# Five more expert blocks computed ahead, the decays behind two rows, the attention heads in two rounds: five reorderings in a two-block transformer kernel

## The reference, cut to what matters

```python
def first_block(x, c, ...):                      # windowed attention + gated linear attention, then PEER
    x = x + gate1 * mixed
    h2 = rms_norm(x, norm2_w) * (1 + scale2) + shift2
    x = x + gate2 * peer_ffn(h2, peer_wq, peer_subkeys, peer_u, peer_v)
    return rms_norm(x, final_norm_w)

def peer_ffn(h, wq, subkeys, u, v):              # 16384 experts, 8 heads, top 16 each
    q = (h @ wq).reshape(B, S, 8, 2, 128)
    sub_scores = einsum('bshpk,hpnk->bshpn', q, subkeys)
    top_v, top_i = top_k(sub_scores, 16)         # per half; sums of pairs; top 16 of 256; softmax = gates
    hid = gelu(einsum('tkd,td->tk', u[expert], x)) * gates
    return einsum('tk,tkd->td', hid, v[expert])

def second_block(x, c, ...):
    x = x + 0.5 * gt1 * swiglu(modulate(x, ...), w1_gate, w1_up, w1_down)
    proj = modulate(x, ...) @ w_in
    y_mla = softmax(mask(q k^T + q_pe k_pe^T)) v @ w_o_mla        # 8 heads, 512 x 512, causal by chunks of 64
    y_gdn = gated_delta_rule(silu(conv(q, k, v)), a, b, z) @ w_o_gdn   # decays from a, b; 8 chunks of 64
    x = x + gt2 * ((gate_mla * y_mla + gate_gdn * y_gdn) @ w_out)
    x = x + 0.5 * gt3 * swiglu(modulate(x, ...), w2_gate, w2_up, w2_down)
    return rmsnorm(x, g_final)
```

## Time and profile before

| | |
|---|---|
| median of three runs | 3515.35 us (3514.06 to 3519.29) |
| profiled execution | 3512.49 us, span of the trace 3510.7 us |
| mean granted TensorE clock | 0.962 |
| busy share of TensorE, VectorE, ScalarE, GpSimd | 94, 58, 38, 15% |
| chain that ended last | TensorE 82%, VectorE 10%, ScalarE 4%, DMA 2%, GpSimd 2% |

### The profile page before, as it was taken

The page is one execution under the profiler, slowest core; times in us unless marked ns, Lnnn a source line. Parts: engine busy times, 40 slices in busy tenths (PEclk is TensorE's granted clock), DMA queues, the critical chain, the costliest instruction groups (busy, mean ns, idle before and its releaser), DMA issues.

```text
span 3510.7 us, 41073 instructions
## 1 busy us (share of the span) xinstructions
PE 3300.3 (94%) x16321; PEld 2728.8 (78%) x16321; DVE 2047.9 (58%) x3543; ACT 1326.3 (38%) x2337; POOL 528.5 (15%) x547
## 2 busy tenths in 40 slices
PE   8999979999999999999999987989898998899998
PEld 5755879998888888888788866778687655678887
DVE  5765987867778888777555335535533344433332
ACT  3131238973444444444322234445442123232221
POOL 0001009962222222221000000000000000000000
PEclk9998999999999999999899998999898999999999
DMA  6416234669999899886355321122121121222222
GB/s 249 145 60 222 73 115 149 220 229 344 322 329 329 318 331 326 323 322 218 123 187 183 134 99 49 64 81 78 54 82 54 38 100 48 90 70 99 96 95 74
DMA packets 188767, 572.45 MB, mean 163 GB/s; under 512 B 16416, under 2 KB 80672, under 8 KB 170272
## 3 DMA queue, kind: packets, MB, share of 16 engines
q1 hardware_dynamic: 150704, 365.99, 29.8%
q0 software_dynamic: 37872, 203.84, 15.9%
HBM read 522.91 MB, written 46.86 MB: 162 GB/s over the span
## 4 chain that ended last, share of the span: by engine, by line
PE 82%; DVE 10%; ACT 4%; DMA 2%; POOL 2%; issue 1%; SPq 0%; DVEq 0%; ACTq 0%; POOLq 0%
PE ps L231 11%; PE ps L232 11%; PE ps L233 11%; PE ps L1601 5%; PE ps L1602 5%; PE ps L1600 5%; PE ps L240 4%; PE ps L1362 4%; PE ps L1364 4%; PE ps L1363 4%; PE ps L581 2%; PE ps L316 2%; DVE Wl L223 1%; PE ps L171 1%; DMA hidden_dram<-peerg_HS 1%; PE ps L584 1%
## 5 line engine op out<-in xcount | busy, mean ns | idle before, releaser
L223 DVE TENSOR_TENSOR Wl<-W,Wh 128x1024 fp32r<-128x1024 f32 x363 | 438.4, 1208 | 697.5 <-ACT Wh L217 697.5
L217 ACT ACTIVATE Wh<-W 128x1024 fp32r<-128x1024 f32 x363 | 377.7, 1041 | 567.0 <-PE ps L233 545.0
L1362 PE MATMUL ps<-peer_Hh,Wh 128*128 128x384 f32 x1024 | 348.9, 341 | 14.1 <-DVE Wl L223 14.1
L1364 PE MATMUL ps<-peer_Hh,Wl 128*128 128x384 f32 x1024 | 345.2, 337 | 0.0
L1363 PE MATMUL ps<-peer_Hl,Wh 128*128 128x384 f32 x1024 | 344.8, 337 | 0.0
L1570 POOL DMA_INDIRECT peerv_UV<-peer_uv,peer_EX x128 | 210.0, 1640 | 655.8 <-DVE peer_Y L1637 606.4
L1600 PE MATMUL ps<-peerv_VH,peer_HTh 128*128 128x512 f32 x768 | 299.9, 391 | 8.2 <-DVE peer_HTl L1663 8.2
L1602 PE MATMUL ps<-peerv_VH,peer_HTl 128*128 128x512 f32 x768 | 301.2, 392 | 0.0
L1601 PE MATMUL ps<-peerv_VL,peer_HTh 128*128 128x512 f32 x768 | 301.2, 392 | 0.0
L231 PE MATMUL ps<-f_Hh,Wh 128*128 128x512 f32 x672 | 262.3, 390 | 2.2 <-DVE Wl L223 2.2
L233 PE MATMUL ps<-f_Hh,Wl 128*128 128x512 f32 x672 | 261.5, 389 | 0.0
(11 more groups left out here) (490 smaller groups left out, 6508.9 us busy)
## 6 DMA issues: line engine op xcount, KB each, us to landing
W<-peer_u SPq DMA_DIRECT2D x128, 512.0 KB, 7.0
peerv_VR<-peer_v SPq DMA_DIRECT2D x128, 512.0 KB
gates_dram<-peerg_GB SPq DMA_DIRECT2D x12, 2048.0 KB, 7.3
peerv_GR<-gates_dram SPq DMA_DIRECT2D x32, 768.0 KB, 8.8
f_AW<-w_ada POOLq DMA_DIRECT2D x48, 512.0 KB, 4.3
W<-w_gate SPq DMA_DIRECT2D x44, 512.0 KB, 3.2
W<-w_up SPq DMA_DIRECT2D x44, 512.0 KB, 3.2
swa_AW<-w_ada POOLq DMA_DIRECT2D x32, 512.0 KB, 4.4
```

Of the source, the lines that this page charges most:

```text
L217: A.then_inc(e.activation(w_parts(i)[0], w_raw(i), ACT.Copy), ("w_hi", i))
L223: V.then_inc(e.tensor_tensor(lo, w_raw(i), hi.bitcast(F32), SUB), ("w", i))
L1362: e.matmul(o, hi[:, k, :], H2[0][:, k, 0:TD], start=k == 0, stop=False)
L1364: ins = e.matmul(o, lo[:, k, :], H2[0][:, k, 0:TD], start=False, stop=k == 7)
```

## The change

It does seven things. (1) `NPRE` becomes 54 and `FIRST` 15; 32 blocks stay between the one-hot products and 7 follow at the end. (2) VectorE's split of expert tiles 1 and 2 moves from the gates stage into the last two steps of the query stage, and the two `behind(e, "query")` go. (3) At the start of the dense stage SP's first two `gr_load` and GpSimd's first three gathers stand ahead of `hidden_written`. (4) The transposes of the decays and what follows on ScalarE and VectorE move behind the first two rows; the splits of row 1 move ahead of the decays. (5) The `uq` fills move one place back, and the eighth goes to `BEHIND`. (6) In the heads, VectorE's five steps are cut in two rounds, and each round has a piece of 6, 6, 3, 6 or 3 matmuls of a branch tile. (7) The first two tiles of `w_out` run their parts 0 to 6 first and part 7 last, each part behind its own wait.

```diff
-    NPRE = 49
+    NPRE = 54
-    NQ, FIRST = 96, 12
+    NQ, FIRST, EARLY = 96, 15, 2
@@ def query_dve(e):
-            if nb < 15:
+            if nb < 15 + EARLY:
                 w_lo(e, (t_q + t_u)[nb + 2])
@@ def gates_dve(e):
-        behind(e, "query")
+        PE.wait_ge(e, ("sub", 15))
         for p in range(FIRST):
-            w_lo(e, t_u[p + 1])
+            if p >= EARLY:
+                w_lo(e, t_u[p + 1])
@@ def dense_sp(e):
         gates_written(e)
-        hidden_written(e)
         gr_load(e, 0)
         gr_load(e, 1)
+        hidden_written(e)
@@ def dense_pool(e):
         gates_written(e)
-        hidden_written(e)
         for k in range(128):
+            if k == 3:
+                hidden_written(e)
             uv_load(e, k)
@@ mix2_pe, mix2_act, mix2_dve: the transposes and all behind "tcv" go into decay_pe, decay_act, decay_dve
+        w_hi(e, t_row[1])
+        w_lo(e, t_row[1])
@@ def rows_pe(e):
                 pe_three(e, ps(n % 2), t_row[n], 8, 128, H4, 0, 8, ("row", n))
+            if n == 1:
+                decay_pe(e)
@@ def rows_act(e): (rows_dve likewise, with w_lo and decay_dve)
-            if n < NROW - 1:
+            if 0 < n < NROW - 1:
                 w_hi(e, t_row[n + 1])
+            if n == 1:
+                decay_act(e)
@@ def delta_pe(e): (the waits of delta_act and delta_dve for "nds" and "tcv" go too)
-        V.wait_ge(e, "tcv")
-        A.wait_ge(e, "tcv")
@@ FILL
-            ([("rope", 0)], [("red", 0), ("bc", 0), ("uq", 0)]),
-            ([("uq", 1), ("on", 0)], [("ot", 0, 0), ("uq", 2)]),
+            ([("rope", 0)], [("red", 0), ("bc", 0)]),
+            ([("uq", 0), ("on", 0)], [("ot", 0, 0), ("uq", 1)]),
...
+        def pieces_pe(self, e, nb):
+            n = len(self.banks)
+            if nb >= n:
+                V.wait_ge(e, (self.tag, "out", nb - n))
+            V.wait_ge(e, ("w", self.ts[nb]))
...
+            for ks in ((0, 1), (2, 3), (4,), (5, 6), (7,)):
+                for k in ks:
+                    e.matmul(o, hi[:, k, :], self.parts[0][:, k, :], start=k == 0, stop=False)
+                    e.matmul(o, hi[:, k, :], self.parts[1][:, k, :], start=False, stop=False)
+                    ins = e.matmul(o, lo[:, k, :], self.parts[0][:, k, :], start=False, stop=k == 7)
+                if k == 7:
+                    PE.then_inc(ins, ("w", self.ts[nb]), (self.tag, "t", nb))
+                yield
@@ def attend_dve(e, h):
             V.then_inc(e.tensor_scalar(st[:, 1:2], st[:, 0:1], -SC_, None, MUL), ("pneg", h, q))
+            yield
             A.wait_ge(e, ("pexp", h, q))
             V.then_inc(e.reciprocal(st[:, 3:4], st[:, 2:3]))
             V.wait_ge(e, V.n)
             P = P_[:, q % 2, 0:w_]
             V.then_inc(e.tensor_scalar(P, P, st[:, 3:4], None, MUL), ("pn", h, q))
-            yield
@@ def branch_pe(e):
-        for r in range(39):
-            if r % 5 == 3:
-                br1.tile_pe(e, r // 5)
-            yield
+        for nb in range(8):
+            for _ in br1.pieces_pe(e, nb):
+                yield
@@ def wout2_pe(e):
-        V.wait_ge(e, ("y", "lo", 7))
-        for nb in range(8):
+        for t, k in [(t, k) for k0 in (0, 7) for t in (0, 1) for k in (range(7) if k0 == 0 else (7,))]:
+            V.wait_ge(e, ("y", "lo", k))
...
+            if k == 7:
+                PE.then_inc(ins, ("w", t_wo2[t]), ("wout2", t))
+        for nb in range(2, 8):
```

More of the change, by code:

```diff
@@ L1955, in mix2_pe, with decay_pe @@
         n4.pe_two(e, [ps(2), ps(3)], t_ab, 8, [("ab", 0), ("ab", 1)])
+    def decay_pe(e):
         V.wait_ge(e, "lx")
@@ L1962, in mix2_pe, with decay_act, decay_dve @@
         PE.then_inc(ins, "tcv")
+    def decay_act(e):
+        PE.wait_ge(e, "tcv")
+        V.wait_ge(e, "tcv")
+        pv = ps(4).rearrange("p (b s h) -> p b s h", b=4, s=16)
+        A.then_inc(e.activation(tcv[:, :, 2, :], pv[:, :, 0, :], ACT.Exp))
+        A.then_inc(e.activation(tcv[:, :, 3, :], pv[:, :, 2, :], ACT.Exp), "tcv")
+    def decay_dve(e):
+        PE.wait_ge(e, "tcv")
+        pv = ps(4).rearrange("p (b s h) -> p b s h", b=4, s=16)
+        V.then_inc(e.tensor_copy(tcv[:, :, 0:2, :], pv[:, :, 0:2, :]), "tcv")
+        V.wait_ge(e, "tcv")
+        V.then_inc(e.tensor_scalar(nds8, tcv[:, :, 0, :], -1.0, None, MUL), "nds")
     def mix2_act(e):
@@ L1976, in mix2_act @@
         A.then_inc(e.activation(ea[0:8, 0:1], vec("a_log")[0:8, :], ACT.Exp), "ea")
-        PE.wait_ge(e, "tcv")
-        V.wait_ge(e, "tcv")
-        pv = ps(4).rearrange("p (b s h) -> p b s h", b=4, s=16)
-        A.then_inc(e.activation(tcv[:, :, 2, :], pv[:, :, 0, :], ACT.Exp))
-        A.then_inc(e.activation(tcv[:, :, 3, :], pv[:, :, 2, :], ACT.Exp), "tcv")
     def mix2_dve(e):
@@ L2005, in mix2_dve @@
                                    SQc[:, :, 63:64].broadcast_to([8, 8, 64]), SQc, SUB), "lx")
-        PE.wait_ge(e, "tcv")
-        pv = ps(4).rearrange("p (b s h) -> p b s h", b=4, s=16)
-        V.then_inc(e.tensor_copy(tcv[:, :, 0:2, :], pv[:, :, 0:2, :]), "tcv")
-        V.wait_ge(e, "tcv")
-        V.then_inc(e.tensor_scalar(nds8, tcv[:, :, 0, :], -1.0, None, MUL), "nds")
     def part(h, c):
@@ L2087, in rows_dve @@
         for n in range(NROW + 2):
-            if n < NROW - 1:
+            if 0 < n < NROW - 1:
                 w_lo(e, t_row[n + 1])
+            if n == 1:
+                decay_dve(e)
             if n - 2 in norm_of:
@@ L2332, in delta_pe @@
     def delta_pe(e):
-        V.wait_ge(e, "tcv")
-        A.wait_ge(e, "tcv")
         row_steps(chain(rows_pe(e), keys_pe(e)), lambda h: head_pe(e, h))
     def delta_act(e):
-        V.wait_ge(e, "nds")
         x_out.wait_ge(e, "x")
@@ L2402, in build @@
             ([("uk", 6)], [("lsq", 0), ("uk", 7)]),
[6 rows of a table removed]
-    BEHIND = [("red", 3), ("uq", 8), ("uv", 0), ("on", 3), ("uq", 9), ("rope", 1), ("uv", 1), ("ot", 3, 0), ("ot", 3, 1),
+            ([("rope", 0)], [("red", 0), ("bc", 0)]),
+            ([("uq", 0), ("on", 0)], [("ot", 0, 0), ("uq", 1)]),
+            ([("uq", 2)], [("ot", 0, 1), ("red", 1), ("uq", 3)]),
+            ([("uq", 4), ("on", 1)], [("ot", 1, 0)]),
+            ([("uq", 5)], [("red", 2), ("ot", 1, 1)]),
+            ([("uq", 6), ("on", 2)], [("ot", 2, 0), ("ot", 2, 1)])]
+    BEHIND = [("red", 3), ("uq", 7), ("uq", 8), ("uv", 0), ("on", 3), ("uq", 9), ("rope", 1), ("uv", 1), ("ot", 3, 0), ("ot", 3, 1),
               ("uv", 2), ("uq", 10), ("rope", 2), ("uv", 3), ("uq", 11), ("rope", 3), ("uv", 4), ("uv", 5), ("rope", 4),
@@ L2663, in tile_pe @@
             pe_three(e, self.bank(nb), self.ts[nb], 8, 128, self.parts, 0, 8, (self.tag, "t", nb))
+        def pieces_pe(self, e, nb):
[3 more added lines that the diff above has]
+            V.wait_ge(e, ("w", self.ts[nb]))
+            hi, lo = (w.rearrange("p (k m) -> p k m", k=8) for w in w_parts(self.ts[nb]))
+            o = self.bank(nb)
+            for ks in ((0, 1), (2, 3), (4,), (5, 6), (7,)):
[6 more added lines that the diff above has]
+                yield
         def tile_act(self, e, nb):
@@ L2851, in wout2_pe @@
     def wout2_pe(e):
-        V.wait_ge(e, ("y", "lo", 7))
-        for nb in range(8):
+        w = [[x.rearrange("p (k m) -> p k m", k=8) for x in w_parts(i)] for i in t_wo2[0:2]]
+        for i in t_wo2[0:2]:
+            V.wait_ge(e, ("w", i))
+        for t, k in [(t, k) for k0 in (0, 7) for t in (0, 1) for k in (range(7) if k0 == 0 else (7,))]:
+            V.wait_ge(e, ("y", "lo", k))
+            o, (hi, lo) = ps(t), w[t]
+            e.matmul(o, hi[:, k, :], YP[0][:, k, :], start=k == 0, stop=False)
+            e.matmul(o, hi[:, k, :], YP[1][:, k, :], start=False, stop=False)
+            ins = e.matmul(o, lo[:, k, :], YP[0][:, k, :], start=False, stop=k == 7)
+            if k == 7:
+                PE.then_inc(ins, ("w", t_wo2[t]), ("wout2", t))
+        for nb in range(2, 8):
             if nb >= 4:
```

## The result

The changed kernel takes **3464.47 us** (median, 3460.65 to 3467.54) against 3514.7 us for the kernel before on the same chip: ratio **0.9856**, 95% interval 0.9839 to 0.9873. The forecast was 3460. The profiled execution took 3464.78 us, span 3463.0. So the total came out 4.5 us above the forecast, but its parts did not all come out, as the following shows.

What follows compares the result with a forecast made beforehand. TensorE was taken as the bound, with only its waits and low clock to remove. The terms -16 - 7 - 5 - 25 - 2.5 = -55.5 us gave 3457 profiled, 3460 us median; range 3447 to 3478, about 8 in 10.

Steps and rivals of the forecast that it cites:

- The bound: Whole kernel: the time is TensorE's own work, its waits and its low clock; the edits remove only waits and slow stretches.
- Parts 1 to 3: Gates and dense stage: blocks moved -20.9, gates' end +8.4, gates' start +3.7, dense start -7.2; -16.0 us, between -7 and -22.
- part 3: Dense start: earlier gathers and gate load leave a wait of 3 in place of 8.2 and no clock loss; -7.2 us.
- Part 4: Decays: two rows under the 11.75 us wait let row 2 start 8.4 us sooner; -7 us, between -3 and -9.
- The sign that the prediction asked for here: Decays: row 2 would stand about 8 us after the transposes of the decays.
- Part 5: `uq` fill: the 6.4 us wait on `QL` leaves 2.8 and the clock loss shrinks; -5 us (-2 to -6.5).
- Part 6: Heads: waits from VectorE's order get covered by the other head's maximum and branch matmuls; -25 us, bounds -11 and -31.
- Part 7: `w_out`: TensorE starts 2.7 us sooner, clock 1.5 kept, new wait of 1.7; net -2.5 us (-5 to +1).
- A: Rival, heads: TensorE's gain is half, through forty switches between kinds of matmul and semaphores; 3472 us, chance 0.16.
- B: Rival, gates: they only shift, the start slips by 8 us and the dense-start gate load stays late; 3470, chance 0.09.
- C: Rival, dense stage: VectorE or a landing stretches pairs of rounds, so TensorE no longer bounds; mostly near 3480, chance 0.05.
- D: Rival: a moved wait binds elsewhere; decays, `uq` fill and `w_out` give 4 in place of 14.5; 3470, chance 0.08.

Runs made afterwards that it cites:

- x4: The kernel before with only the first three parts (54 blocks ahead, early split, loads ahead of the writes' wait): 3499.69 us, 0.9956.
- x9: The kernel before with only the dense stage's loads of gates and expert rows ahead of the wait for the hidden rows' writes: 3505.0 us, 0.9974.
- x7: The changed kernel with 63 expert blocks ahead instead of 54: 3463.77 us, 0.9857 against the kernel before.
- x10: The kernel before with only the early split of the first two tiles and the later start of the list: 3507.23 us, 0.9982.
- x2: The kernel before with only the decays moved behind two rows: 3510.41 us, 0.9994.
- x5: The kernel before with only VectorE's head work in two rounds, branch tiles whole: 3510.99 us, 0.9991.
- x6: The kernel before with only the branch's tiles in pieces, VectorE's head work in one round: 3487.72 us, 0.993.
- x11: The changed kernel with row 0's convolution ahead of the decay chain and w_out's first two tiles one after the other: 3454.87 us, 0.9831 against the kernel before.
- x1: The changed kernel with the move of the decays undone: 3465.48 us, 0.9862 against the kernel before.
- x8: The changed kernel with row 0's convolution ahead of VectorE's decay chain and the decays' transposes behind row 2: 3461.33 us, 0.9851 against the kernel before.
- x12: The changed kernel with the lists `FILL` and `BEHIND` as before: 3465.87 us, 0.9867 against the kernel before.
- x3: The kernel before with both edits of the heads, VectorE's two rounds and tiles in pieces: 3484.77 us, 0.9913.

## Why the prediction was right, and where it was not

**The bound.** TensorE stayed the bound everywhere, and all gains are waits and clock, as the first step said. The range held, and the sign was never in doubt.

**Parts 1 to 3, -16.0 forecast, -12.5 in the trace** (x4: -14.1). The unit price of 4.19 us a block held: the dense stage is 21.7 us shorter (forecast 20.9). The mis-sized terms are the start and the tail, and as one trace scatters, all of them are used here. From the first hidden block to the last one-hot product it is 305.5 to 310.8 us in the six kernels with the old start, and 312.0 to 313.2 in the seven with the new one: 4.9 us more by the middle ones, where 3.7 was forecast. The wait behind the second early split came out at 4.5 us where I had 6.5, but three blocks fill only the 3.5 us on the chosen gates, and the 3.42 us on GpSimd's one-hots stay. From the last one-hot product to the end of the dense stage it is 892.9 to 893.8 us in six kernels with the old code and 874.6 to 875.7 in six with the new: 18.0 shorter, where 20.9 - 8.4 + 7.2 = 19.7 was forecast. x9 alone gives 6.5 of it for part 3 (forecast 7.2). The changed kernel's own tail misleads: 46.7 us against 42.8, 3.9 more where 8.4 - 7.2 = 1.2 was forecast, but it is the longest of the six (the others 44.2 to 45.3). Behind its wait of 1.98 us on a split one block ran at a lower clock and took 1.65 us more than the next:

```profile
783.14:788.95 5.81, 5.81 (x25) 5.81 (x25) 1.23 (x1) 0.33 (x1) 0.00 (x0) 0.71 1.01 420
788.95:793.11 4.16, 4.16 (x26) 4.16 (x25) 1.23 (x1) 1.44 (x2) 0.00 (x0) 1.00 0.97 372
```

The sum hid a simpler truth that x7 and x9 plus x10 show: moving blocks is neutral, and only the two reorderings of waits pay. (The bounds given for parts 1 to 3, -7 and -22, are -6.0 and -22.7 when their terms are added; nothing hangs on it.)

**Part 4, -7 forecast, about -1 to -2 measured. This step failed.** I asked what is late next, and answered "row 2 behind row 0's convolution"; row 2 indeed starts 6.3 us sooner, once the 13.3 us by which `t_ab` already was ahead are taken off. But the step ended there, and not at the next place where the path waits for the convolutions. Counted from `t_ab`, row 0's convolution is 7.6 us sooner, row 1's 3.3 (2111.52 - 2072.60 against 2128.09 - 2085.87), the seventh 0.15. Three things were missed: VectorE has row 0's convolution behind its decay chain, so that the norm of row 0 holds TensorE for 4.8 us in front of row 2; ScalarE has the `exp` of the decays in front of row 0's root, which holds VectorE for 2.93 us in place of 0.27 ahead of row 1's convolution; and the rows behind run at a lower clock (0.81 in place of 0.91). My lower bound of -3 was no bound. The sign that the prediction asked for here came true and did not tell: row 2 stands 8.0 us behind the transposes (2107.51 - 2099.54).

**Part 5, -5 forecast, -5.7 in its own stage, of which 4.2 are the fill's; -2.6 with the heads.** The wait came as drawn, 2.76 us left of 6.45 (forecast 2.8). The mis-sized term is the clock's return: the 12 passes after the wait took 7.11 us where they had taken 7.39, and I had given back 1.5. That the stage as a whole still came out near the forecast is luck: 1.5 us come with the clock at its start, which x2 has without the new fill. The loss in the heads, 1.6 to 1.8 us of clock, was not thought of.

**Part 6, -25 forecast, -28.7 measured** (in the changed kernel 114.9 us from first scores to second branch, 2969.98 - 2855.09, against 143.6). The size was nearly right, for a reason that was half wrong: I put VectorE's order first and called the tiles the cover. x5 shows that the order alone gives 1.6 us, and x6 that the pieces alone give 26.1. The term that I left too small is the clock: TensorE's busy time for the same matmuls fell by 8.7 us, and I had counted all waits and clock losses as one.

**Part 7, -2.5 forecast, -1.5 in its stage, nothing in the rest of the trace.** Both waits came as drawn, 2.56 and 1.86 us (forecast 2.5 and 1.7). x11 shows that the new one was avoidable. From the last cut of the heads' output to the first product of squares it is 67.4 us in place of 68.9, but from there to the end 426.4 in place of 425.0, with the same instructions (the same in x1 and x7; 425.1 and 425.6 in x8 and x12). No run has this edit alone, so that it saves time on the whole is not shown.

**The sum.** In the trace's span: -12.5 (parts 1 to 3), -0.2 (decays), -5.7 (state), -28.7 (heads), -1.5 (`w_out`), that is -48.6 where -55.5 was forecast; 2.1 us were gained ahead of the first hidden block and 3.0 lost in stretches that nobody touched (1.3 of them between the dense stage and `t_ab`, 1.4 behind `w_out`), which leaves -47.7. The 6.9 us of difference are the decays (6.8 too much), parts 1 to 3 (3.5 too much), `w_out` (1.0 too much), the heads (3.7 too little) and the state (0.7 too little): the misses partly cancelled, so that the total came out this near is in part luck.

**The rivals.** A (heads at half) is refuted by x3 and x6: the pieces between attention matmuls cost nothing that shows (110.71 us busy in the changed heads, where the prediction counted 111 of work). B came in part: the dense start was good, the gates' start slipped by 4.9. C is refuted with room to spare: x7 has a distance of two everywhere, 338 GB/s, and 1.5 us of idle time in 792. D came true in the decays, where it took nearly the whole part; in `w_out` the new wait was no longer than forecast.

The 358 GB/s that the prediction took from the Trainium skill (DMA: Bandwidth & Descriptors, "Where 436 GB/s comes from") as what the memory gives one core was no bound here. Over the dense stage the kernels stay below it (338 GB/s in x7), but at the dense start two windows of 12 us, of the kernel before and of the changed one, show more:

```profile
808.00:820.00 12.00, 12.00 (x46) 9.94 (x47) 9.85 (x12) 4.09 (x10) 3.35 (x2) 0.81 1.01 413
```

```profile
816.00:828.00 12.00, 10.74 (x52) 9.10 (x52) 10.04 (x14) 4.76 (x10) 3.36 (x2) 1.00 1.02 411
```

The measurement decides. Another page of the Trainium skill (Perfetto Trace Analysis, "Roofline") says that a core that works alone can draw more than its share, up to about 435 GB/s of its 16 DMA engines; this kernel runs on one core, and with that page the rival would have had only a token chance.

## What to carry to other kernels

When an engine waits in short pieces, put filler work of the same size into each of these rounds before reordering the engines it waits for: spreading whole tiles into pieces gave 26 us where reordering gave 1.6, and the reordering paid only afterwards, 3 to 4 us. Moving work between two stages in which the bounding engine is full gains nothing, however large the stage's own difference looks. And when a gain is booked at the first instruction behind a removed wait, follow the path to the next place where it waits for the same engine: of 7.6 us at row 0, 0.15 was left at the seventh convolution in the changed kernel's trace, and 1 to 2 us in the medians.
